# Decoder layer in fp32 on one core: the modulation rows of the first half move from VectorE to TensorE (four column strips), the low parts of h from GpSimd to VectorE, and TensorE gets 40 matmuls of constants to run early

## The chip, the cores and the metric

The kernel runs on one core of a Trainium2 chip. The metric is the device time in microseconds of one execution, as the median of several. TensorE (PE) has its own queue of instructions, and so have VectorE (DVE), ScalarE (ACT), GpSimd (POOL) and SyncE (SP), which here issues the loads. The engines meet only through semaphores, so the order of instructions on each engine is the order in which the Python code emits them.

## The reference

One layer over x of 1024 tokens by 1024 features, in float32. A conditioning vector c gives six rows of 1024 (shift, scale and gate, twice):

```python
mod = jax.nn.silu(c) @ w_ada[l] + b_ada[l]
shift1, scale1, gate1, shift2, scale2, gate2 = [m[:, None, :] for m in jnp.split(mod, N_MOD, axis=-1)]
h = rms_norm(x, norm_attn[l]) * (1.0 + scale1) + shift1
proj = h @ w_in[l]
...                                  # two attention groups, output projection, gate1, residual
h = rms_norm(x, norm_ffn[l]) * (1.0 + scale2) + shift2
ffn = (jax.nn.silu(h @ w_gate[l]) * (h @ w_up[l])) @ w_down[l]
x = x + gate2 * ffn
```

Only the part up to the first projections is touched: shift1 and scale1 (2048 columns of `w_ada`), the norm of x, h, and the first two of the 18 column tiles of `h @ w_in`.

## The kernel before, in words

Features lie on partitions: `x_in` is 8 chunks (j = 0 to 7) of 128 features by 1024 tokens. Each engine has one function, and the order in it is written by hand. A product in full precision is made of three fp32r matmuls: an operand is split into a high part (`hH`, `WH`, a copy rounded to fp32r) and a low part (`hL`, `WL`, the difference), and `three` (L1506 to L1508) adds high by high, high by low and low by high.

The stretch before the steady projections, called the prelude here, goes like this.

1. VectorE works out the angles of the rotary embedding (L938 to L962). ScalarE squares the chunks of x as they land (L569), and VectorE adds the squares (L980). PE turns the sums (L1537, fp32 transposes), VectorE reduces them (L1003, L1005), GpSimd raises the mean to the power -0.5 (L484), VectorE puts the result on diagonals (`diagonals`, L968), and PE spreads it over all partitions (`broadcast`, two fp32 matmuls of 128x512, L1531) into PSUM banks 6 and 7.
2. The 2048 columns of shift1 and scale1 come in four groups g = 0 to 3 of 512 columns, each good for two chunks of h. VectorE's `adaln1(g)` adds up seven of the eight products of `silu_c` with the weights (L990, L995: one tensor_scalar and six scalar_tensor_tensor of 128x512). PE's `adaln1(g)` sums over partitions and adds the eighth product, with 8 fp32 matmuls of one column (L1551, L1552). VectorE's `scale_shift(g)` (L1013, L1016) makes `mod1` and `a1` of it.
3. For each chunk j, VectorE multiplies x by the broadcast (L1021). ScalarE makes h with scale `a1` and bias `mod1` in place (L577), then `hH` as a copy of it (L579). GpSimd makes `hL` (L491).
4. PE runs the first two tiles of the projection against the chunks as they come (`half_chunk(0, ...)` on chunk n, `half_chunk(1, ...)` on chunk n - 3; 6 matmuls each). The remaining 16 tiles are whole (`proj_tile`, L1517), 48 matmuls each.

Behind the prelude GpSimd clears `acc2`, which lies over `x_in`, once all `hL` are made (L494). SyncE then loads the first piece of the other 4096 columns (`ada2`, L361), and VectorE's `ada_step` (L1039) takes it into `acc2`. On VectorE `ada_step(0)` stands between `wsplit(2)` and `wsplit(3)`; the latter makes `WL` of tile 3, for which PE waits at its start (semaphore `split_l`). Later in the layer come the attention groups and the FFN, which the change leaves as they are.

Of the kernel before, what the change touches and what calls it, by code (L numbers as in the profile page):

```python
# [15 lines left out]
F32 = mybir.dt.float32  # L16
# [7 lines left out]
P = 128  # L24
# [72 lines left out]
NM, NS = MH // 2 * NU, SBH // 2 * NU  # L97
BLOCKS = [NT - i for _, i in UNITS]
# [11 lines left out]
def build(nc, xT, cols_d, rows_d, grow_d, pos_d, ada1_d, ada2_d, win_d, qup_d, kvup_d, wout_d, gu_d, down_d, x2_d, t_d, out_d):  # L110
# [17 lines left out]
    silu_c = at("silu_c", [P, KD], F32, 6.125)  # L128
    mod1 = at("mod1", [P, 16], F32, 6.25)
# [134 lines left out]
    names = """small_in pool_const trig_args trig_done silu_c_done x_sq x_add x_turned stat_ms stat_r stat_diag stat_bc acc1_done mod1_mm a1_done  # L264
# [193 lines left out]
    def _(pool):  # L458
# [8 lines left out]

        fill(pool.memset(ident[:], 0.0))
# [82 lines left out]
    def _(act):  # L551
# [12 lines left out]
        A(silu_c[:], cols[:, C_C:C_C + KD], ACT.Silu).then_inc(sem["silu_c_done"], 1)  # L564
        for j in range(KD):
# [364 lines left out]
    def _(dve):  # L930
# [10 lines left out]
        for tt in range(NT):  # L941
            ch(V.tensor_scalar(ang[:, tt, 0, :], fr, pos_f[:, tt:tt + 1], None, ALU.mult))
            ch(V.tensor_scalar(ang[:, tt, 1, :], fr, pos_f[:, tt:tt + 1], None, ALU.mult))
# [38 lines left out]
        def adaln1(g, between=None):  # L982

            if g == 0:
                dve.wait_ge(sem["silu_c_done"], 1)
            if g >= 2:
                dve.wait_ge(sem["mod1_mm"], g - 1)
            dve.wait_ge(ada1_in[g], 16)
            a = acc1[g % 2]
            ch(V.tensor_scalar(a[:], ada1[:, g, 0, :], silu_c[:, 0:1], None, ALU.mult))  # L990
            for k in range(1, KD - 1):
                if k == 4 and between:
                    between()
# [12 lines left out]
        diagonals(0, 0, diag1)  # L1006
        adaln1(0)
# [491 lines left out]
    def _(pe):  # L1499
# [40 lines left out]
        def adaln1(g):  # L1540
# [6 lines left out]
            pe.wait_ge(sem["silu_c_done"], 1)  # L1547
            pe.wait_ge(sem["acc1_done"], g + 1)
            for m in range(4):
                w = slice(m * P, (m + 1) * P)  # L1550
                mm(ps[:, 4 + g % 2, m:m + 1], ada1[:, g, KD - 1, w], silu_c[:, KD - 1:KD], start=True, stop=False, skip_group_check=True)  # L1551
                last = mm(ps[:, 4 + g % 2, m:m + 1], acc1[g % 2][:, w], ones[:, 0:1], start=False, stop=True, skip_group_check=True)  # L1552
            last.then_inc(sem["mod1_mm"], 1)

        broadcast(0, diag1, 6)
        adaln1(0)


# [8 lines left out]
        for n in range(KD + LAG):  # L1567
            if n % 2 == 0 and n // 2 + 1 < KD // 2:
                adaln1(n // 2 + 1)
            if n < KD:  # L1570
                pe.wait_ge(sem["hL_done"], n + 1)
                for hf in range(2):
                    last = half_chunk(0, 0, hf, n, hH, hL)
                if n == KD - 1:
                    last.then_inc(sem["pe_tile"], 1)
            if n >= LAG:
                for hf in range(2):
                    last = half_chunk(1, 2, hf, n - LAG, hH, hL)
# [426 lines left out]
```

## Time and profile before

| | before |
|---|---|
| median of 3 runs | 1446.08 us (1443.46 to 1449.19) |
| profiled execution: its own time | 1443.19 us |
| its span, first to last instruction | 1441.2 us |
| PE busy | 1326.0 us, 92% |
| VectorE busy | 833.1 us, 58% |
| ScalarE busy | 547.3 us, 38% |
| GpSimd busy | 84.5 us, 6% |
| mean granted TensorE clock | 0.971 |

The span is shorter than the execution's time by 2.0 us, which lie around it. The profiled execution is 2.9 us under the median. In the page, "PEclk" is the clock granted to TensorE as a share of 2.4 GHz: 1.00 is that level, 0.50 is 1.2 GHz. Starts and durations of a timeline are in microseconds from the start of the span.

### The profile page before, as it was taken

What the parts mean: (1) busy time and instruction counts of PE and PEld (TensorE: products, weight loads), DVE (VectorE), ACT (ScalarE), POOL (GpSimd) and SP (SyncE); (2) the same over time, 40 slices, a digit from 0 to 9 for tenths busy, and PEclk for the clock granted to TensorE, in tenths of its full rate; (3) what the DMA queues carried; (4) which work ended last, traced back from release to release, by engine and by line L of the source; (5) the groups of instructions that cost most, each with busy time, mean ns of one, the idle gap of its engine ahead of it and who ended that gap; (6) DMA issues with size and microseconds to landing.
All of it is one profiled execution on the core that took longest, in us unless ns stands there. A gap on an engine that the chain in (4) does not pass through costs nothing.

```text
span 1441.2 us, 17190 instructions
## 1 busy us (share of the span) xinstructions
PE 1326.0 (92%) x6624; PEld 1107.3 (77%) x6624; DVE 833.1 (58%) x1225; ACT 547.3 (38%) x883; POOL 84.5 (6%) x82
## 2 busy tenths in 40 slices
PE   2899999887989898969989999999999999999998
PEld 1688878776877777768867788888888877887886
DVE  8633354477565998865368755666566633334333
ACT  3522312356444776852136333333333322323231
POOL 1600200132000000010000000000000000001001
PEclk9799999899999999979999999999999999999999
DMA  9053423000003323500122122222222225446443
GB/s 383 31 212 124 161 102 121 15 0 1 1 1 74 76 50 74 183 30 17 57 99 106 74 88 88 88 88 88 88 74 74 72 77 201 154 137 242 161 146 124
DMA packets 37404, 143.47 MB, mean 100 GB/s; under 512 B 4176, under 2 KB 4304, under 8 KB 35792
## 3 DMA queue, kind: packets, MB, share of 16 engines
q1 hardware_dynamic: 34992, 134.03, 27.5%
q0 software_dynamic: 2336, 8.39, 1.6%
q8 instruction: 52, 0.85, 0.3%
q14 instruction: 24, 0.20, 0.0%
HBM read 112.00 MB, written 19.92 MB: 92 GB/s over the span
## 4 chain that ended last, share of the span: by engine, by line
PE 71%; DVE 16%; issue 6%; ACT 3%; POOL 2%; DMA 1%; DVEq 0%; SPq 0%; ACTq 0%; POOLq 0%
PE ps L1905 26%; PE ps L1517 15%; PE ps L1506 8%; PE ps L1508 8%; PE ps L1507 8%; DVE left L1243 5%; PE ps L1713 2%; DVE acc L995 1%; DVE beta L1248 1%; PE ps L1702 1%; POOL rstd L508 1%; PE ps L1735 1%; PE ps L1722 1%; DMA t_spill_d<-tst 1%; PE ps L1822 1%
## 5 line engine op out<-in xcount | busy, mean ns | idle before, releaser
L1506 PE MATMUL ps<-TH,dWH 128*128 128x512 f32 x352 | 137.8, 391 | 7.2 <-DVE dWL L1474 6.3
L1507 PE MATMUL ps<-TL,dWH 128*128 128x512 f32 x352 | 137.7, 391 | 0.0
L1508 PE MATMUL ps<-TH,dWL 128*128 128x512 f32 x352 | 137.6, 391 | 0.0
L1905 PE MATMUL ps<-h2H,slH 128*128 128x512 f32 x320 | 124.6, 389 | 2.4 <-ACT s L900 2.4
L1905 PE MATMUL ps<-h2L,slH 128*128 128x512 f32 x320 | 124.5, 389 | 0.0
L1905 PE MATMUL ps<-h2H,slL 128*128 128x512 f32 x320 | 124.5, 389 | 0.0
L1472 DVE TENSOR_TENSOR TL<-traw,TH 128x512 fp32r<-128x512 f32 x44 | 30.5, 693 | 138.6 <-ACT TH L921 138.6
L883 ACT ACTIVATE slH<-ssum 128x512 fp32r<-128x512 f32 x80 | 50.4, 632 | 146.3 <-PE ps L1905 96.2
L1243 DVE TENSOR_TENSOR_SCAN left<-omb 128x127 f32<-128x127 f32 (+3 forms) x64 | 86.3, 1348 | 13.7 <-ACT omb L783 13.7
L921 ACT ACTIVATE TH<-traw 128x512 fp32r<-128x512 f32 x44 | 27.8, 631 | 168.9 <-PE ps L1508 156.8
L974 DVE TENSOR_TENSOR WL<-raw,WH 128x1024 fp32r<-128x1024 f32 x30 | 38.3, 1280 | 85.9 <-ACT WH L561 85.9
L1506 PEld LDWEIGHTS ps<-TH,dWH 128*128 128x128 f32 x352 | 66.5, 189 | 22.3 <-issue 7.1
L1517 PE MATMUL ps<-hH,WH 128*128 128x512 f32 x256 | 79.6, 392 | 0.0
L1517 PE MATMUL ps<-hL,WH 128*128 128x512 f32 x256 | 78.9, 389 | 0.0
L1517 PE MATMUL ps<-hH,WL 128*128 128x512 f32 x256 | 78.8, 389 | 0.0
L1508 PEld LDWEIGHTS ps<-TH,dWL 128*128 128x128 f32 x352 | 66.5, 189 | 13.8
L1507 PEld LDWEIGHTS ps<-TL,dWH 128*128 128x128 f32 x352 | 66.4, 189 | 13.8
L1735 PE MATMUL ps<-VS,wT 128*128 128x64 f32 x576 | 75.1, 278 | 0.0
L1735 PEld LDWEIGHTS ps<-VS,wT 128*128 128x128 f32 x576 | 73.4, 201 | 0.0
L1905 PEld LDWEIGHTS ps<-h2H,slH 128*128 128x128 f32 x320 | 60.1, 188 | 15.3 <-DVE slL L1419 2.8
L1905 PEld LDWEIGHTS ps<-h2L,slH 128*128 128x128 f32 x320 | 60.1, 188 | 12.4
L1905 PEld LDWEIGHTS ps<-h2H,slL 128*128 128x128 f32 x320 | 60.1, 188 | 12.4
(296 smaller groups left out, 3021.3 us busy)
## 6 DMA issues: line engine op xcount, KB each, us to landing
ada<-ada SPq DMA_DIRECT2D x12, 2048.0 KB, 8.1
draw<-down SPq DMA_DIRECT2D x44, 512.0 KB, 3.6
sraw<-gu SPq DMA_DIRECT2D x20, 1024.0 KB, 5.9
traw<-t_spill_d SPq DMA_DIRECT2D x44, 256.0 KB, 3.8
t_spill_d<-tst SPq DMA_DIRECT2D x20, 512.0 KB, 3.0
raw<-win SPq DMA_DIRECT2D x18, 512.0 KB, 3.7
x_in<-xT SPq DMA_DIRECT2D x4, 1024.0 KB, 8.5
headKH<-pairKH SPq DMA_DIRECT2D x16, 256.0 KB, 4.9
```

The lines of the kernel that those rows point to most:

```text
L883: A(slH[q][:], operand(u, q), ACT.Copy).then_inc(sem["g_h"], 1)
L921: A(TH[d % 2][:], traw[d % 2][:], ACT.Copy).then_inc(sem["th_done"], 1)
L974: V.tensor_tensor(WL[par % 2][:], raw[r % 2][:], WH[par % 2][:], ALU.subtract).then_inc(sem["split_l"], 1)
L1243: V.tensor_tensor_scan(left[v % 2][:, 1:n], omb[v % 2][:, 0:n - 1], omb[v % 2][:, 0:n - 1], 1.0, ALU.mult, ALU.bypass).then_inc(sem["s_sca ...
L1472: V.tensor_tensor(TL[d % 2][:], traw[d % 2][:], TH[d % 2][:], ALU.subtract).then_inc(sem["tl_done"], 1)
L1506: mm(out, lh, rh, start=first, stop=False)
L1507: mm(out, lh, rl, start=False, stop=False)
L1508: return mm(out, ll, rh, start=False, stop=last)
L1517: last = mm(ps[:, b + hf, :], l[s][:, j * P:(j + 1) * P], r[:, j, 512 * hf:512 * hf + 512], start=(j == 0 and k == 0), stop=(j == KD - 1 a ...
L1713: last = mm(ps[:, 6 + v % 2, 0:VD], pmT[v % 2][:, k * P:(k + 1) * P], VM[:, qt + k, (2 * i + e) * VD:(2 * i + e + 1) * VD], start=(k == 0) ...
L1735: last = mm(ps[:, bank, c:c + SBD], wT[v % 2][:, k * P:(k + 1) * P], VS[:, qt + k, (2 * i + e) * SBD:(2 * i + e + 1) * SBD], start=(k == 0 ...
L1905: last = mm(ps[:, Q_BANK[q], :], l[q][:, w], r[:, c, :], start=(c == 0 and k == 0 and q not in (Q_G2, Q_S4)), stop=(c == 3 and k == 2), sk ...
```

## The change

- VectorE no longer adds up the modulation rows. PE does it (`mod1_rows(g)`): eight fp32 matmuls, whose stationary operand `silu_w` has 32 columns per k (silu(c) in the first, zeros in the others) and whose moving operand is 128x512 of the weights. Matmul k writes the 32 partitions 32*(k % 4) onward of one PSUM bank, so it uses one of four column strips of the array, two matmuls to a strip. VectorE copies the bank to SBUF (`mod1_copy`), and PE sums over partitions with four fp32 matmuls of one column (`mod1_columns`), where there were eight.
- `hL` is made by VectorE (`h_low`) instead of GpSimd.
- ScalarE makes `hH` straight from x with scale and bias, and h after it, with the same scale and bias; before, `hH` was a copy of h.
- The 16 small instructions for the angles become two. The eight small ones for the first diagonals become two halves, and each half of the broadcast has a wait and a signal of its own. `wsplit(0)` moves behind the reduction, `wsplit(1)` behind the diagonals.
- PE runs 40 bf16 matmuls of 128x128 on a constant (`WARM`) between the transposes and the first `mod1_rows`.
- In the loop of the first two tiles, PE no longer takes the three kinds of products of a chunk together: the four matmuls that need only `hH` come as soon as that is there, then `mod1_rows`, the chunk of tile 1, `mod1_columns`, and last the two with `hL`.

```diff
+WARM = 40
...
-        for j in range(KD):
-            pool.wait_ge(sem["hH_done"], j + 1)
-            nc.gpsimd.tensor_tensor(hL[:, j, :], x_in[:, j, :], hH[:, j, :], ALU.subtract).then_inc(sem["hL_done"], 1)
...
+            A(hH[:, j, :], x_in[:, j, :], ACT.Identity, scale=a1[:, j:j + 1], bias=mod1[:, j:j + 1]).then_inc(sem["hH_done"], 1)
             A(x_in[:, j, :], x_in[:, j, :], ACT.Identity, scale=a1[:, j:j + 1], bias=mod1[:, j:j + 1]).then_inc(sem["h_done"], 1)
-            act.wait_ge(sem["h_done"], j + 1)
-            A(hH[:, j, :], x_in[:, j, :], ACT.Copy).then_inc(sem["hH_done"], 1)
...
+        def mod1_copy(g):
+
+            dve.wait_ge(sem["ada_part"], g + 1)
             if g >= 2:
                 dve.wait_ge(sem["mod1_mm"], g - 1)
...
+            V.tensor_copy(acc1[g % 2][:], ps[:, 4 + g % 2, :]).then_inc(sem["acc1_done"], 1)
...
+        def normalize(j):
+            V.tensor_tensor(x_in[:, j, :], x_in[:, j, :], pair(6), ALU.mult).then_inc(sem["xr_done"], 1)
+
+        def h_low(j):
+            dve.wait_ge(sem["hH_done"], j + 1)
+            dve.wait_ge(sem["h_done"], j + 1)
+            V.tensor_tensor(hL[:, j, :], x_in[:, j, :], hH[:, j, :], ALU.subtract).then_inc(sem["hL_done"], 1)
+
+        mod1_copy(0)
+        dve.wait_ge(sem["stat_bc"], 2)
+        normalize(0)
+        scale_shift(0)
+        normalize(1)
         for g in range(KD // 2):
...
+            if 2 * g + 2 < KD:
+                normalize(2 * g + 2)
+            h_low(2 * g)
             if g + 1 < KD // 2:
...
+                mod1_copy(g + 1)
+                normalize(2 * g + 3)
+            h_low(2 * g + 1)
+            if g + 1 < KD // 2:
+                scale_shift(g + 1)
...
+        def mod1_rows(g):
+
             if g == 0:
                 pe.wait_ge(sem["stat_ms"], 1)
+                pe.wait_ge(sem["silu_c_done"], 2)
             if g >= 2:
                 pe.wait_ge(sem["a1_done"], g - 1)
             pe.wait_ge(ada1_in[g], 16)
...
+            for k in range(KD):
+                c = k % 4
+                last = mm(ps[32 * c:32 * c + 32, 4 + g % 2, :], silu_w[:, k, :], ada1[:, g, k, :], start=(k < 4), stop=(k >= 4))
+            last.then_inc(sem["ada_part"], 1)
```

On PE, from the end of the transposes to the second group, the row of instructions before was this (`diag` is the diagonal, `ada` the weights of the modulation, `acc` the row sums; two numbers behind a name are the program's buffer number):

```order
L1537 MATMUL ps<-ident,sqs 128x128 x7
L1531 MATMUL ps<-diag_97,ones 128x512 [waits stat_diag]
L1531 MATMUL ps<-diag_97,ones 128x512
L1551 MATMUL ps<-silu_c,ada_90 128x1 [waits silu_c_done,acc1_done,ada1_in0,stat_ms]
L1552 MATMUL ps<-ones,acc_91 128x1
...
L1551 MATMUL ps<-silu_c,ada_90 128x1 [waits silu_c_done,acc1_done,ada1_in1,split_l]
L1552 MATMUL ps<-ones,acc_92 128x1
...
L1506 MATMUL ps<-hH,WH_79 128x512 [waits hL_done]
L1507 MATMUL ps<-hL,WH_79 128x512
L1508 MATMUL ps<-hH,WL_81 128x512
```

and of the change it is this:

```order
L1541 MATMUL ps<-ident,sqs 128x128 x7
L1565 MATMUL ps<-identb 128x128 x40
L1554 MATMUL ps<-ada_91,silu_w 32x512 [waits ada1_in0,silu_c_done,stat_ms]
L1554 MATMUL ps<-ada_91,silu_w 32x512 x7
L1569 MATMUL ps<-diag_98,ones 128x512 [waits stat_diag] x2
L1561 MATMUL ps<-ones,acc_92 128x1 [waits acc1_done]
L1561 MATMUL ps<-ones,acc_92 128x1 x3
L1587 MATMUL ps<-hH,WH_80 128x512 [waits hH_done,split_l]
L1587 MATMUL ps<-hH,WH_80 128x512
L1587 MATMUL ps<-hH,WL_82 128x512 x2
L1554 MATMUL ps<-ada_91,silu_w 32x512 [waits ada1_in1]
L1554 MATMUL ps<-ada_91,silu_w 32x512 x7
```

The constants and eight matmuls of the rows now stand ahead of the broadcast, and the rows of group 1 stand behind the first chunk's `hH` products, where the one-column matmuls of group 1 stood ahead of everything of chunk 0.

On VectorE, one turn of the loop over groups was this before (`mod` and `a` are `mod1` and `a1`):

```order
L1021 TENSOR_TENSOR x_in<-x_in,ps 128x1024 x2
L990 TENSOR_SCALAR acc_91<-ada_90,silu_c 128x512 [waits ada1_in2,mod1_mm]
L995 SCALAR_TENSOR_TENSOR acc_91<-ada_90,silu_c,acc_91 128x512 [waits dve] x3
L1013 TENSOR_TENSOR mod_60<-ps,cols 128x2x2 [waits mod1_mm]
L1016 SCALAR_TENSOR_TENSOR a_61<-mod_60,cols 128x2 [waits dve]
L995 SCALAR_TENSOR_TENSOR acc_91<-ada_90,silu_c,acc_91 128x512 [waits dve] x3
```

and is this with the change:

```order
L1009 TENSOR_TENSOR x_in<-x_in,ps 128x1024
L1014 TENSOR_TENSOR hL<-x_in,hH 128x1024 [waits h_done,hH_done]
L986 COPY acc_92<-ps 128x512 [waits mod1_mm,ada_part]
L1009 TENSOR_TENSOR x_in<-x_in,ps 128x1024
L1014 TENSOR_TENSOR hL<-x_in,hH 128x1024 [waits h_done,hH_done]
L1003 TENSOR_TENSOR mod_61<-ps,cols 128x2x2 [waits mod1_mm]
L1006 SCALAR_TENSOR_TENSOR a_62<-mod_61,cols 128x2 [waits dve]
```

The seven accumulations are gone. A copy that waits for PE and two `hL` that wait for ScalarE have come in, and the scale and shift of the next group stand at the end of the turn.

## Rows read from the trace of the kernel before

**Rows 1.** The page: shares of the chain that ended last, by engine

```profile
PE 71%; DVE 16%; issue 6%; ACT 3%; POOL 2%; DMA 1%; DVEq 0%; SPq 0%; ACTq 0%; POOLq 0%
```

**Rows 2.** Windows of PE alone: stretch, length, busy (instructions), granted clock, DMA share, GB/s

```profile
33.40:36.00 2.60, 1.12 (x6) 0.51 0.96 410
...
47.00:50.40 3.40, 1.92 (x13) 0.99 0.00 0
50.40:57.00 6.60, 6.60 (x21) 0.51 0.01 2
...
61.70:77.00 15.30, 15.25 (x67) 1.00 0.24 75
```

**Rows 3.** Timeline, 3 to 38 us: start, duration, engine, line, instruction, count

```profile
3.78 0.24 DVE L942 TENSOR_SCALAR ang<-rows,pos_f 128x32 f32<-128x32 f32 x1
...
10.54 9.20 DVE L980 TENSOR_TENSOR sqs<-sqs,sq 128x1024 f32<-128x1024 f32 x7
...
17.18 1.06 ACT L569 ACTIVATE sq<-x_in 128x1024 f32<-128x1024 f32 x1 [0.27 <-DVE sqs L980]
...
19.89 1.94 PE L1537 MATMUL ps<-ident,sqs 128*128 128x128 f32 x8 [19.89 <-DVE sqs L980]
...
23.51 1.68 POOL L484 TENSOR_TENSOR rms<-ms,nhalf 128x8 f32<-128x8 f32 x1 [20.48 <-DVE ms L1005]
...
26.93 3.50 PE L1531 MATMUL ps<-diag,ones 128*128 128x512 f32 x4 [5.10 <-DVE diag L968]
...
37.12 0.16 DVE L1016 SCALAR_TENSOR_TENSOR a<-mod,cols 128x2 f32<-128x2 f32 x1
```

**Rows 4.** Groups by form, 0 to 80 us: count, busy, mean ns, idle before

```profile
L995 DVE SCALAR_TENSOR_TENSOR acc<-ada,silu_c,acc 128x512 f32<-128x512 f32 x24 | 22.0, 916 | 0.7
...
L577 ACT ACTIVATE x_in<-x_in,mod,a 128x1024 f32<-128x1024 f32 x8 | 9.9, 1235 | 27.5 <-DVE a L1016 27.5
L1021 DVE TENSOR_TENSOR x_in<-x_in,ps 128x1024 f32<-128x1024 f32 x8 | 9.4, 1213 | 0.0
```

**Rows 5.** Timeline, 59 to 87 us

```profile
59.41 0.36 PE L1552 MATMUL ps<-ones,acc 128*128 128x1 f32 x2
59.64 0.36 PE L1551 MATMUL ps<-silu_c,ada 128*128 128x1 f32 x2
...
61.42 0.29 DVE L1016 SCALAR_TENSOR_TENSOR a<-mod,cols 128x2 f32<-128x2 f32 x1
...
69.03 3.53 POOL L494 MEMSET acc<- 128x4096 f32 x1
...
76.84 0.62 PE L1517 MATMUL ps<-hH,WH 128*128 128x512 f32 x2
...
80.61 4.49 DVE L1039 SCALAR_TENSOR_TENSOR acc<-ada,silu_c,acc 128x4096 f32<-128x4096 f32 x1 [6.63 <-DMA ada<-ada]
85.01 1.22 DVE L974 TENSOR_TENSOR WL<-raw,WH 128x1024 fp32r<-128x1024 f32 x1
```

**Rows 6.** Timeline of PE at full clock: four fp32 matmuls of 128x512, then bf16

```profile
209.21 3.59 PE L1531 MATMUL ps<-diagl,ones 128*128 128x512 f32 x8
...
393.15 0.23 PE L1676 MATMUL ps<-mask_mla,identb 128*128 128x128 bf16 x1
393.21 0.71 PE L1702 MATMUL ps<-ident,pm 128*128 128x128 f32 x5
```

**Rows 7.** Groups by form, whole span: the nearest row to VectorE's new copy

```profile
L1182 DVE COPY pmT<-ps 128x384 f32<-128x384 f32 x8 | 4.5, 558 | 0.1
```

**Rows 8.** What reads or writes x_in and ada: issues (from, to), time to landing (min/median/max)

```profile
L349 SPq DMA_DIRECT2D x_in<-xT x4: 434/469/688, 2.1 to 3.6; - x4
...
DMA to landing us min/median/max: 5.4/8.5/11.5
...
L353 SPq DMA_DIRECT2D ada<-ada x4: 457/668/1201, 5.4 to 7.3; - x4
...
DMA to landing us min/median/max: 17.3/24.3/30.6
```

More of the change, by code:

```diff
@@ L940, in _ @@
         fr = rows[:, R_FREQ:R_FREQ + HALF]
[L941 to L943 removed]
+        for c in range(2):
+            ch(V.tensor_tensor(ang[:, :, c, :], fr.unsqueeze(1).broadcast_to([P, NT, HALF]), pos_f[:].unsqueeze(2).broadcast_to([P, NT, HALF]), ALU.mult))
         ch.sync()
@@ L1005, in _ @@
         V.tensor_scalar(ms[:, 0, :], rss[:], 1.0 / D, EPS, ALU.mult, ALU.add).then_inc(sem["stat_ms"], 1)
-        diagonals(0, 0, diag1)
-        adaln1(0)
+        wsplit(0, 0)
+        dve.wait_ge(sem["stat_r"], 1)
+        for hf in range(2):
+            t = slice(4 * hf, 4 * hf + 4)
+            V.tensor_tensor(diag1[:, t, :], ident[:].unsqueeze(1).broadcast_to([P, 4, P]), rms[:, 0, t].unsqueeze(2).broadcast_to([P, 4, P]), ALU.mult).then_inc(sem["stat_diag"], 1)
+        wsplit(1, 1)
         def scale_shift(g):
@@ L1546, in adaln1, with mod1_columns @@
             pe.wait_ge(ada1_in[g], 16)
-            pe.wait_ge(sem["silu_c_done"], 1)
+            for k in range(KD):
+                c = k % 4
+                last = mm(ps[32 * c:32 * c + 32, 4 + g % 2, :], silu_w[:, k, :], ada1[:, g, k, :], start=(k < 4), stop=(k >= 4))
+            last.then_inc(sem["ada_part"], 1)
+        def mod1_columns(g):
             pe.wait_ge(sem["acc1_done"], g + 1)
             for m in range(4):
-                w = slice(m * P, (m + 1) * P)
-                mm(ps[:, 4 + g % 2, m:m + 1], ada1[:, g, KD - 1, w], silu_c[:, KD - 1:KD], start=True, stop=False, skip_group_check=True)
-                last = mm(ps[:, 4 + g % 2, m:m + 1], acc1[g % 2][:, w], ones[:, 0:1], start=False, stop=True, skip_group_check=True)
+                last = mm(ps[:, 4 + g % 2, m:m + 1], acc1[g % 2][:, m * P:(m + 1) * P], ones[:, 0:1], start=True, stop=True)
             last.then_inc(sem["mod1_mm"], 1)
-        broadcast(0, diag1, 6)
-        adaln1(0)
+        for _ in range(WARM):
+            mm(ps[:, 0, 0:P], identb[:], identb[:], start=True, stop=True)
+        mod1_rows(0)
+        for hf in range(2):
+            pe.wait_ge(sem["stat_diag"], hf + 1)
+            mm(ps[:, 6 + hf, :], ones[:], diag1[:, 4 * hf:4 * hf + 4, :].rearrange("p t n -> p (t n)"), start=True, stop=True).then_inc(sem["stat_bc"], 1)
+        mod1_columns(0)
         def in_pair(t0, i):
@@ L1567, in _ @@
         for n in range(KD + LAG):
-            if n % 2 == 0 and n // 2 + 1 < KD // 2:
-                adaln1(n // 2 + 1)
+            if n < KD:
+                w = slice(n * P, (n + 1) * P)
+                pe.wait_ge(sem["hH_done"], n + 1)
+                for k, l in enumerate((WH, WL)):
+                    for hf in range(2):
+                        mm(ps[:, hf, :], l[0][:, w], hH[:, n, 512 * hf:512 * hf + 512], start=(n == 0 and k == 0), stop=False)
+            if n % 2 == 0 and n // 2 + 1 < KD // 2:
+                mod1_rows(n // 2 + 1)
+            if n >= LAG:
+                for hf in range(2):
+                    last = half_chunk(1, 2, hf, n - LAG, hH, hL)
+            if n % 2 == 0 and n // 2 + 1 < KD // 2:
+                mod1_columns(n // 2 + 1)
             if n < KD:
@@ L1572, in _ @@
                 for hf in range(2):
-                    last = half_chunk(0, 0, hf, n, hH, hL)
+                    last = mm(ps[:, hf, :], WH[0][:, w], hL[:, n, 512 * hf:512 * hf + 512], start=False, stop=(n == KD - 1))
                 if n == KD - 1:
                     last.then_inc(sem["pe_tile"], 1)
-            if n >= LAG:
-                for hf in range(2):
-                    last = half_chunk(1, 2, hf, n - LAG, hH, hL)
         last.then_inc(sem["pe_tile"], 1)
```

35 lines of the change are left out of this document (8 added, 27 removed).

## The prediction

> **What bounds the kernel now.** I read the shares of the chain that ended last first: TensorE holds 71% of it and VectorE 16% [rows 1]. The windows of PE and the timeline of the first 90 us then say where that differs. From 61.75 us on PE goes without a gap, 67 matmuls in 15.25 us, 0.227 us each [rows 2], and it hands over to the whole tiles at 76.84 us [rows 5]. Those are bound by PE and the change leaves them alone. So what the change can move is the moment 76.84, and what hangs on it a little later.
>
> Ahead of 61.75 us VectorE is the bound. `a1` of group 0 is ready at 37.28 us and that of group 3 at 61.71 us [rows 3, 5]. That is 24.4 us over three groups, 8.1 us each on the mean (9.8 us for the first two, less for the last, whose scale and shift stand early). In a group VectorE makes six scalar_tensor_tensor at 0.916 us on the mean and two products at 1.213 us [rows 4], with a tensor_scalar and two small ones. Idle time before these rows is nearly nothing, so VectorE is at work all through. At 61.7 us PE still has 66 of the 96 matmuls of tiles 0 and 1 before it. This is a backlog, and it matters below: it was 15.1 us of work from 61.75 to 76.84.
>
> **The new operation, and its price R.** The eight matmuls of `mod1_rows` are fp32 with 512 moving columns. At full clock four such matmuls are recorded as 8 pieces in 3.59 us [rows 6], the drain of the last included, so a piece takes 0.427 us and a matmul 0.854 us. At 26.93 us two of them took 3.50 us [rows 3], that is 0.85 us a piece: half speed. No row of before has a matmul that uses 32 columns of the array. The bounds for R at full clock are:
> - one after another, as the broadcasts go: 8 x 0.854 = 6.83 us
> - all four strips at once: two rounds of 0.854 us, 1.7 us, and 1.9 us with some filling.
>
> I take a value between: every fp32 matmul is two pieces, all rows of PE show starts in program order, and the second piece of a strip cannot start before the first of the same strip is done. If a later strip may not pass it, its first piece runs beside the earlier strip's second, so two pieces are in flight: 8 x 0.427 + 0.427 = 3.84 us. I keep both ends for the range.
>
> The Trainium skill (TensorE: Matmul & The Clock Gate, Part 3: Packing small matmuls) says that matmuls start and end strictly in order, and that three column tiles of 512 columns gave 2.38 times the speed. The first speaks for 3.84 us. By the second, taken to four tiles as 3.1 times, an estimate from that page, R would be 2.2 us and the kernel near 1437 us. No run here shows either yet.
>
> **Up to `a1` of group 0.** The 16 small instructions, 0.24 us each [rows 3], become two of 256 columns, at most 0.56 us each (a copy of 384 [rows 7]). The first add of squares can start up to 1 us sooner than 10.54 us. The last chunk of x lands at 3.6 + 11.5 = 15.1 us [rows 8]. Two squares (1.06 us each) and one add (1.22 us, as every difference of 1024 columns [rows 5]) behind it, with their waits, end near 18.7 us. The seven adds ended at 19.74 us [rows 3], so this gains 1.0 us. The transposes (1.94 us), reduction and rsqrt follow at the same distance: `rms` at 24.2 us instead of 25.19 [rows 3]. `wsplit(0)` lies beside GpSimd's 1.68 us and costs nothing. The two halves of the diagonals (0.69 each, as the copy below) end at 25.6 us. `wsplit(1)` ends at 26.8 us, before the rows are done, hidden too.
>
> PE starts the 40 constants at 20.9 us. A bf16 matmul of 128x128 is followed after 0.06 us at full clock [rows 6]: 2.4 us at full clock, 4.8 us at half. I take 25.2 us for their end, since PE was idle before. The weights of group 0 landed at 5.4 + 17.3 = 22.7 us, the last group's at 7.3 + 30.6 = 37.9 us [rows 8], in time for every group here. Then:
> - rows 3.84 us to 29.04
> - broadcast, 2 x 0.854 to 30.75
> - end of PE's pipe and semaphore 0.27 (a matmul of 0.227 us is recorded as 0.39)
> - `normalize(0)` 1.21 to 32.2
> - scale and shift 0.35 to 32.6 us.
>
> The copy and the one-column matmuls (four at 0.225 us [rows 5], 0.9 us) lie beside the broadcast and `normalize(0)`. So `a1` of group 0 comes at 32.6 us, 4.7 us earlier.
>
> **One group.** The path goes: `a1`, ScalarE's `hH` 1.24 us [rows 4] with 0.08 for the semaphore, four matmuls 0.91, rows R, pipe 0.27, copy 0.69 (0.558 us for 384 columns [rows 7], carried to 512), `normalize` 1.17, `h_low` 1.17, scale and shift 0.35, semaphore 0.1. This is 5.98 + R. The one-column matmuls (0.9 + 0.27) lie beside the two VectorE instructions that follow the copy. ScalarE needs 4 x 1.24 = 4.96 us a group, VectorE 2 x 1.17 + 2 x 1.17 + 0.69 + 0.35 = 5.7 us, so neither is the bound. With R = 3.84 a group takes 9.82 us and `a1` of group 3 comes at 32.6 + 29.5 = 62.0 us, no earlier than the 61.71 of before.
>
> **From there to the end of tile 1.** PE has a smaller backlog now. Behind `a1` of group 3 stand 1.3 us for `hH` of chunk 6, 42 matmuls (the rest of chunks 6 and 7 of tile 0 and chunks 3 to 7 of tile 1), 9.5 us, and about 0.5 us of waits on the last `hL`: 11.3 us instead of 15.1. Tile 1 ends at 73.3 us, 3.5 us earlier than 76.84.
>
> **What is late next.** GpSimd clears `acc2` only when the last `hL` is made, in 3.53 us, then the load of `ada2` takes 8.05 us, from 72.56 to 80.61 us, `ada_step(0)` 4.49 us, and only behind it comes `wsplit(3)`, done at 86.23 us [rows 5]. PE wants that at the end of tile 2: 76.84 + 48 x 0.227 = 87.7 us. Before there were 1.5 us to spare. Now the last `hL` comes at 62.0 + 0.1 + 4 x 1.24 + 0.1 + 1.2 = 68.4 us (ScalarE makes two pairs behind `a1`). Then 3.6 + 8.05 + 4.49 + 1.2 us bring `WL` of tile 3 at 85.8 us, and tile 2 ends at 73.3 + 10.9 = 84.2 us. PE waits 1.5 us. After that the steps follow the tiles again.
>
> The sum is 3.5 - 1.5 = 2.0 us faster. On the profiled execution's 1443.19 us this gives 1441.2 us. The median of the runs stands 2.9 us above that execution, so I predict 1446.08 - 2.0 = **1444 us**. What a measurement of this kernel can tell from no change is about 0.5%, 7.2 us.
>
> **The rivals.**
> 1. *Four strips at once, R = 1.9.* `a1` of group 0 at 30.65 us, groups of 7.88 us, group 3 at 54.3, tile 1 at 65.6, and the wait of 1.5 us: 9.7 us faster, 1436.4 us. For it: strips share no columns and no output partitions. Against it: program order, and two pieces to each matmul. The estimate of 1437 by the page's speedup ends near it.
> 2. *The strips don't overlap, R = 6.83.* This is the one on the other side. `a1` of group 0 at 35.6 us, groups of 12.81 us, group 3 at 74.0, tile 1 at 85.3: 10 us slower, 1456 us. For it: all 6,000 and more other matmuls go one by one. It decides from R near 4.5: each us of R costs 1 + 3 = 4 us, so the gain of 2.0 is gone at R = 4.34.
> 3. *PE at the lower clock in the loop.* The granted clock was at 0.51 from 33.4 and again from 50.4 us, each time after a stretch in which PE had been idle or had done one-column matmuls (in 47.0 to 50.4 us it was busy 1.92 of 3.40 us) [rows 2]. Now each group has 0.9 us of one-column work and gaps of 1.1 us for the copy and 1.2 us for `hH`. Behind `mod1_columns(0)` the gap is 2 us. A group at half speed adds 3.84 + 0.91 = 4.75 us, all three 14 us: 1458 us. Against it: the rest of each group is dense. The constants speak only of the start. Without the 2.4 GHz level at 25.2 us the first rows and the broadcast cost 5.5 us more.
>
> **How the numbers follow.** Two strips at a time: 0.45, near 1444, own range 1439 to 1449. Four at once or close to it (R under 3): 0.28. No overlap: 0.14. Low clock in most groups: 0.08. The remaining 0.05 is for something else, on either side. Two in ten may lie outside: the range goes from 1434 (the first rival and its fill at nothing) to 1455 us. Faster by over 0.5% needs R near 2.5 or less, 0.28 of the first rival and a little of the rest: 0.30. Slower by over 0.5% is rivals 2 and 3: 0.21. Within: 0.49.
>
> **What would show it.** In the profile of the change: the time from the first to the last piece of eight matmuls with `silu_w` (1.9, 3.8 or 6.8 us); whether pieces of neighbouring strips overlap; `a1` at 32.6 us and then every 9.8 us; the first whole tile at 73.3 us; VectorE idle before the copy in each group, waiting for PE; PE idle for 1.5 us before tile 3, until `WL`. The granted clock should be at 1.00 from 25 us on. The prediction is wrong if R is far from 3.84, if the clock falls in the loop, or if ScalarE's `hH` with scale and bias is slower than 1.24 us.

## The result, and the profile after

| | runs | median us | lowest to highest | profiled run: time, span, granted clock |
|---|---|---|---|---|
| before | 6 | 1448.18 | 1443.46 to 1450.22 | 1443.19, 1441.2, 0.971 |
| changed | 6 | 1435.22 | 1431.80 to 1438.66 | 1431.80, 1430.0, 0.983 |

The ratio is 0.9916, 95% interval 0.9892 to 0.9939. The kernel is 12 us (0.84%) faster by the ratio, which is more than the 0.5% that can be told from no change. The forecast was 1444 us and no change. So the forecast of no change failed, although the measured time lies inside the range of 1434 to 1455 us. It lies there because the range reached down to the first rival (1436.4 us, from a base 2.1 us lower), and not because the expected mechanism came true.

The step R is decided by the timeline of the changed kernel from 20 to 31 us (start, duration, engine, line, instruction, count, and in brackets the idle time before with its releaser):

```profile
20.17 1.94 PE L1541 MATMUL ps<-ident,sqs 128*128 128x128 f32 x8 [20.17 <-DVE sqs L979]
21.90 4.03 PE L1565 MATMUL ps<-identb 128*128 128x128 bf16 x40
23.73 2.51 POOL L487 TENSOR_TENSOR rms<-ms,nhalf 128x8 f32<-128x8 f32 x1 [20.47 <-DVE ms L991]
25.86 0.16 PEld L1554 LDWEIGHTS ps<-ada,silu_w 128*32 128x32 f32 x8
25.86 1.92 PE L1554 MATMUL ps<-ada,silu_w 128*32 128x512 f32 x16
...
26.32 0.13 PEld L1554 LDWEIGHTS ps<-ada,silu_w 128*32 128x32 f32 x4 [0.30 <-issue]
26.75 0.13 PEld L1554 LDWEIGHTS ps<-ada,silu_w 128*32 128x32 f32 x4 [0.30 <-issue]
27.72 1.98 PE L1569 MATMUL ps<-diag,ones 128*128 128x512 f32 x4
...
29.54 0.95 PE L1561 MATMUL ps<-ones,acc 128*128 128x1 f32 x8
31.07 0.16 DVE L1006 SCALAR_TENSOR_TENSOR a<-mod,cols 128x2 f32<-128x2 f32 x1
```

The eight matmuls of `mod1_rows` (16 pieces, L1554) take 1.92 us, where 3.84 us had been taken. The weight loads (PEld) show how: eight at 25.86, then four at 26.32 and four at 26.75, 0.46 and 0.43 us apart, about one piece's 0.427 us. So four pieces of 512 columns run at once, one in each strip, and the pieces of a strip follow each other without a gap. `a1` of group 0 is ready at 31.23 us. In [rows 3] it was 37.28.

Then the groups. From the same timeline, the rows of groups 1 to 3 and their copies:

```profile
34.69 3.64 PE L1554 MATMUL ps<-ada,silu_w 128*32 128x512 f32 x16
38.40 0.69 DVE L986 COPY acc<-ps 128x512 f32<-128x512 f32 x1 [3.37 <-PE ps L1554]
41.46 0.16 DVE L1006 SCALAR_TENSOR_TENSOR a<-mod,cols 128x2 f32<-128x2 f32 x1
44.13 1.92 PE L1554 MATMUL ps<-ada,silu_w 128*32 128x512 f32 x16
46.12 0.69 DVE L986 COPY acc<-ps 128x512 f32<-128x512 f32 x1 [0.70 <-PE ps L1554]
49.19 0.16 DVE L1006 SCALAR_TENSOR_TENSOR a<-mod,cols 128x2 f32<-128x2 f32 x1
52.09 1.92 PE L1554 MATMUL ps<-ada,silu_w 128*32 128x512 f32 x16
```

From one `a1` to the next it takes 10.4, 7.7 and 8.0 us. The prediction's sum for a group, 5.98 + R, gives 7.90 with the measured R. The last two groups agree with it. Group 1 doesn't: its rows took 3.64 us. The windows of PE tell why (stretch, length, busy, granted clock, DMA share, GB/s):

```profile
25.86:27.72 1.86, 1.86 (x19) 1.00 0.99 423
29.54:32.71 3.17, 0.95 (x9) 0.91 1.02 434
32.71:38.40 5.69, 5.62 (x20) 0.50 0.96 397
38.40:69.08 30.68, 28.27 (x148) 0.99 0.07 18
```

After 3.17 us in which PE had 0.95 us of one-column work, TensorE's clock is at the 1.2 GHz level (0.50) for the 5.69 us of group 1, and back at 2.4 GHz behind it. That is the third rival, in one group of three and for 2.5 us instead of 4.75.

Last, what was late behind `a1` of group 3 (57.14 us), again from the timeline. The rows of before are in [rows 5]:

```profile
63.42 3.54 POOL L493 MEMSET acc<- 128x4096 f32 x1 [37.18 <-DVE hL L1014]
69.08 0.62 PE L1521 MATMUL ps<-hH,WH 128*128 128x512 f32 x2
69.28 1.03 ACT L585 ACTIVATE lowT<-ps 128x1024 f32<-128x1024 f32 x1 [2.04 <-PE ps L1512]
74.93 4.49 DVE L1043 SCALAR_TENSOR_TENSOR acc<-ada,silu_c,acc 128x4096 f32<-128x4096 f32 x1 [7.36 <-DMA ada<-ada]
79.34 1.22 DVE L973 TENSOR_TENSOR WL<-raw,WH 128x1024 fp32r<-128x1024 f32 x1
80.70 0.70 PE L1521 MATMUL ps<-hH,WH 128*128 128x512 f32 x2 [0.58 <-DVE WL L973]
92.01 1.03 ACT L585 ACTIVATE lowT<-ps 128x1024 f32 x1 [9.78 <-PE ps L1521]
```

PE goes over to the whole tiles at 69.08 us instead of 76.84. Then it waits for `WL` of tile 3: from the eviction of tile 2 to that of tile 3 are 11.75 us (80.26 to 92.01), to the next one 10.88, a loss of 0.87 us. At tile 3's eviction, at 98.90 us in before, the gain is 6.9 us.

VectorE was busy 54.41 us up to 61.71 us in before. In the changed kernel it is 39.66 us, although it now makes `hL` too. Its share of the chain that ended last is 14% (16% in [rows 1]), PE's 72%.

### The profile page after: what moved, and what is told of

Same layout as the page of the kernel before. It is cut to its first block, busy times and chain, and to the rows that moved or that the text cites. A ratio compares the mean times of both kernels' runs of the same rounds, so it can differ in the third digit from the quotient of the medians.

```text
span 1430.0 us, 17295 instructions
## 1 busy us (share of the span) xinstructions
PE 1321.2 (92%) x6696; PEld 1096.7 (77%) x6696; DVE 820.3 (57%) x1189; ACT 547.9 (38%) x884; POOL 66.2 (5%) x75
## 4 chain that ended last, share of the span: by engine, by line
PE 72%; DVE 14%; issue 6%; ACT 3%; DMA 2%; POOL 2%; DVEq 0%; SPq 0%; ACTq 0%; POOLq 0%
PE ps L1927 26%; PE ps L1521 14%; PE ps L1510 8%; PE ps L1512 8%; PE ps L1511 8%; DVE left L1247 5%; PE ps L1735 2%; DVE beta L1252 1%; PE ps L1724 1%; POOL rstd L507 1%; PE ps L1744 1%; PE ps L1554 1%; DMA t_spill_d<-tst 1%; PE ps L1844 1%; DMA x_in<-xT 1%
## 5 line engine op out<-in xcount | busy, mean ns | idle before, releaser
L1247 DVE TENSOR_TENSOR_SCAN left<-omb 128x127 f32<-128x127 f32 (+3 forms) x64 | 86.3, 1349 | 12.4 <-ACT omb L783 12.4
L1757 PE MATMUL ps<-VS,wT 128*128 128x64 f32 x576 | 71.8, 271 | 0.0
L1757 PEld LDWEIGHTS ps<-VS,wT 128*128 128x128 f32 x576 | 70.0, 193 | 0.0
```

What stands on the lines that cost most here:

```text
L1247: V.tensor_tensor_scan(left[v % 2][:, 1:n], omb[v % 2][:, 0:n - 1], omb[v % 2][:, 0:n - 1], 1.0, ALU.mult, ALU.bypass).then_inc(sem["s_sca ...
L1757: last = mm(ps[:, bank, c:c + SBD], wT[v % 2][:, k * P:(k + 1) * P], VS[:, qt + k, (2 * i + e) * SBD:(2 * i + e + 1) * SBD], start=(k == 0 ...
```

## The experiments

Times are medians. The ratios are to runs of before on the same chip, whose medians lie between 1447.6 and 1448.9 us. Below, "tile 1" is the start of its eviction, the `lowT` row at 69.28 us in the changed kernel (77.04 in before), and "tile 3" likewise (92.01, 98.90). The constant matmuls that some kernels add write to a part of `ps` that holds nothing at that time.

### How many strips

**e1_one_by_one**, no strips, the whole array for each matmul:

```
-    silu_w = at("silu_w", [P, KD, 32], F32, 138)
+    silu_w = at("silu_w", [P, KD, P], F32, 138)
-                c = k % 4
-                last = mm(ps[32 * c:32 * c + 32, 4 + g % 2, :], silu_w[:, k, :], ..., start=(k < 4), stop=(k >= 4))
+                last = mm(ps[:, 4 + g % 2, :], silu_w[:, k, :], ..., start=(k == 0), stop=(k == KD - 1))
```

> The changed kernel with one edit: the stationary operand of the rows has 128 columns (silu(c) in the first, zeros in the others), so each of the eight matmuls uses the whole width and all write the same partitions. Theory (the gain comes from four strips in flight at once; each us of R, the time of eight such matmuls, costs one in the start and one in each of three groups): R goes from 1.9 to 6.8 us at full clock, the first whole tile starts at 69.1 + 4 x 5.0 = 89 us, the kernel takes about 20 us more than the changed one and is slower than before by 7 to 10 us. Rival (strips do not matter, the gain comes from VectorE's freed time): R stays near 1.9 to 2.5, tile 2 starts at 69 to 71 us.

1452.61 us (10 runs), ratio 1.0035 [1.0018, 1.0051]: slower than before. PE's timeline of this kernel:

```profile
25.08 7.08 PE L1553 MATMUL ps<-ada,silu_w 128*128 128x512 f32 x16
32.00 1.88 PE L1568 MATMUL ps<-diag,ones 128*128 128x512 f32 x4
```

R is 6.9 us (25.08 to 32.00). `a1` of group 0 is ready at 35.41 us, where the second rival's sum had 35.6. Tile 1 ends at 87.32 us, 18.0 later than in the changed kernel, for 5.0 us of R. By "4 us for each us of R" it should be 20. The profiled changed kernel had lost 2.5 us in its group 1 to the clock (10.4 for 7.9), and this one 1.5 (14.4 for the sum's 12.9), so the sum becomes 19. This one's transposes also started 0.7 us sooner (19.44 for 20.17), which leaves 18.3.

The slowdown against before is 4.5 us, less than the 7 to 10 expected. This kernel has every other edit of the change, from the angles to the order of the loop. So with the rows on PE, all of them together don't make the kernel faster without the strips. What one does by itself was tried for `hL` only (e7, e10).

**e2_two_strips**, two strips of 64 columns:

```
-    silu_w = at("silu_w", [P, KD, 32], F32, 138)
+    silu_w = at("silu_w", [P, KD, 64], F32, 138)
-                c = k % 4
-                last = mm(ps[32 * c:32 * c + 32, ...], ..., start=(k < 4), stop=(k >= 4))
+                c = k % 2
+                last = mm(ps[64 * c:64 * c + 64, ...], ..., start=(k < 2), stop=(k >= KD - 2))
```

> The changed kernel with two column strips of 64 columns in place of four of 32. Theory (all strips of a round run at once): four rounds of 0.854 us, R = 3.4 us at full clock, tile 2 starts near 69.1 + 4 x 1.6 = 75.5 us, about 6 us more than the changed kernel. Rival (only two pieces are ever in flight, and R = 1.9 comes from something else): R stays at 1.9 with two strips and the time is that of the changed kernel.

1443.98 us (10 runs), ratio 0.9973 [0.9953, 0.9993]; `a1` of group 0 at 32.23 us, tile 1 at 74.41. PE's timeline:

```profile
25.14 3.65 PE L1554 MATMUL ps<-ada,silu_w 128*64 128x512 f32 x16
28.72 1.99 PE L1569 MATMUL ps<-diag,ones 128*128 128x512 f32 x4
```

This kernel has by its construction the overlap that the prediction gave to four strips, two pieces in flight. R is 3.6 us and `a1` of group 0 is 0.4 us from the forecast of 32.6. The median is the forecast's 1444, but from a base of 1448.1 and not 1446.1: the gain is some 4 us, where the forecast had 2.0.

**e12_same_strip_pairs**, four strips, but the two matmuls of a strip follow each other in the program. If starts in program order blocked the strips behind, this order would be the worst one.

```
-                c = k % 4
-                last = mm(..., start=(k < 4), stop=(k >= 4))
+                c = k // 2
+                last = mm(..., start=(k % 2 == 0), stop=(k % 2 == 1))
```

> The changed kernel with one edit: matmul k of the rows goes to strip k // 2 instead of k % 4, so the two of a strip follow each other in program order. Theory (matmuls start in program order and one that waits for its strip blocks those behind it): only neighbours of different strips overlap, R becomes at least 2 x 0.854 + 3 x 0.854 = 4.3 us and at most 5.6 us instead of 1.9, tile 2 starts 10 us or more later than in the changed kernel. Rival (each strip takes its own matmuls in its own time): R stays at 1.9 and nothing changes.

1433.45 us (4 runs), ratio 0.9911 [0.9881, 0.9942]. PE's timeline, with the loads:

```profile
24.84 0.18 PEld L1554 LDWEIGHTS ps<-ada,silu_w 128*32 128x32 f32 x8
24.84 1.94 PE L1554 MATMUL ps<-ada,silu_w 128*32 128x512 f32 x16
25.30 0.15 PEld L1554 LDWEIGHTS ps<-ada,silu_w 128*32 128x32 f32 x4 [0.28 <-issue]
26.72 1.98 PE L1569 MATMUL ps<-diag,ones 128*128 128x512 f32 x4
```

1.94 us against 1.92: the order makes no difference, where blocking would have made it at least 4.3 us. R over the three layouts is 6.9, 3.6 and 1.9 us for one, two and four strips. It goes with the number of strips, and not with their order.

### TensorE's clock

**e3_no_warm** leaves the 40 constants out:

```
-WARM = 40
+WARM = 0
```

> The changed kernel without the 40 constants of 128x128 ahead of the first rows. Theory (they buy the clock for the first rows and the broadcast): the first rows take 3.6 us instead of 1.9 and the broadcast 3.5 instead of 2.0, but they start 2 us sooner, when the mean square is ready; a1 of group 0 comes 1 to 2 us later and tile 2 starts at 70 to 73 us. Rival (the constants are not needed, the transposes before them are enough): a1 of group 0 comes earlier or at the same time, tile 2 at 67 to 69 us.

1438.54 us (5 runs, 1433.25 to 1442.34), ratio 0.9918 [0.9893, 0.9943]. PE's timeline:

```profile
22.62 3.64 PE L1554 MATMUL ps<-ada,silu_w 128*32 128x512 f32 x16 [1.63 <-DMA ada<-ada]
...
34.20 2.37 PE L1554 MATMUL ps<-ada,silu_w 128*32 128x512 f32 x16
```

The rows run at half speed, but they start 3.2 us sooner, as soon as their weights have landed, because no constants stand ahead of them. `a1` of group 0 comes at 30.75 us instead of 31.23, and tile 1 at 67.55.

That doesn't mean that the constants are worth nothing. In this profile x landed sooner, and with it the whole start. The first square of x, first in the changed kernel, then here:

```profile
8.46 1.06 ACT L570 ACTIVATE sqs<-x_in 128x1024 f32<-128x1024 f32 x1 [4.30 <-DMA x_in<-xT]
```

```profile
7.41 1.06 ACT L570 ACTIVATE sqs<-x_in 128x1024 f32<-128x1024 f32 x1 [3.08 <-DMA x_in<-xT]
```

The transposes follow this square after 11.6 to 11.7 us in every profile of the changed kernel and its variants, so here they start 1.1 us sooner (19.05 for 20.17). From their start to `a1` of group 0 are 11.70 us here, and 10.6 to 11.5 us in the seven profiles that have the constants and four strips. So the constants buy 0.2 to 1.1 us. The prediction had them at 5.5 us, and had left out that without them the rows start earlier and lie beside the wait for `rms`.

**e4_fill** puts 36 constants into the gap behind `mod1_columns(0)`, ahead of the group in which the clock was at 0.50:

```
         mod1_columns(0)
+        for _ in range(FILL):      # FILL = 36
+            mm(ps[:, 0, 0:P], identb[:], identb[:], start=True, stop=True)
```

> The changed kernel with 36 more constants behind the one-column matmuls of group 0, in the gap of 2.2 us in which PE waits for hH of chunk 0. Theory (the sparse stretch of PE from 29.5 to 32.7 us is what drops the clock for group 1, where the rows took 3.64 us): the rows of group 1 take 1.9 us, the granted clock stays at 1.00, tile 2 starts 2.5 to 3 us earlier, near 66.3 us. Rival (the fall to half has another cause, such as the narrow matmuls of the rows themselves): the rows of group 1 still take 3.6 us and tile 2 starts at 69 us.

1433.43 us (4 runs), ratio 0.9897 [0.9871, 0.9923]. PE's timeline:

```profile
29.97 2.17 PE L1573 MATMUL ps<-identb 128*128 128x128 bf16 x36
...
33.42 1.92 PE L1555 MATMUL ps<-ada,silu_w 128*32 128x512 f32 x16
```

Group 1 takes 7.8 us instead of 10.4, at a granted clock of 1.00, and tile 1 ends at 66.31 us, 3.0 sooner. The median is 1.8 us below that of the changed kernel, within the spread of either. By itself this profile doesn't show that the fill did it, as the next run says.

**a1_after_again** is the changed kernel once more, on another chip:

> The changed kernel again, unchanged, for more runs of it beside the next kernel on the same chip. Both theories expect 1433 to 1436 us, and a first whole tile that starts at 68 to 69.5 us.

1434.75 us (6 runs), ratio 0.9916 [0.9897, 0.9935]. PE's timeline, and below it the window of group 1 (columns: stretch, length, then busy time of PE, its loads, VectorE, ScalarE and GpSimd, then granted clock, DMA share, GB/s):

```profile
28.88 1.05 PE L1561 MATMUL ps<-ones,acc 128*128 128x1 f32 x8 [0.26 <-DVE acc L986]
31.81 0.70 PE L1587 MATMUL ps<-hH,WH 128*128 128x512 f32 x2 [1.88 <-ACT hH L578]
32.90 1.92 PE L1554 MATMUL ps<-ada,silu_w 128*32 128x512 f32 x16
```

```profile
32.70:38.50 5.80, 4.99 (x34) 2.68 (x32) 4.80 (x7) 2.65 (x4) 0.00 (x0) 1.00 0.96 398
```

The same program keeps the clock at 1.00 this time. Tile 1 ends at 65.75 us, 3.5 us before the first profile and sooner than the 68 to 69.5 expected, and 0.15 us from the 65.6 of the first rival. So the drop in group 1 comes in some runs and not in others. It is the usual case, though: of the eight profiles with four, two or one strips and without the fill, six have it (all but a1 and e12), and the two with the fill, e4 and e8, don't. The rows of group 1 took 3.64 us in the first profile, 2.37 in e3, 3.37 in e7 and 2.38 in e11, where those of group 2 took 1.92; in e1 it was 8.72 for 7.03 us, in e2 4.66 for 3.65. PE's idle time ahead of the first `hH` product is not the same in all. It is 2.2 us in five of the six (2.23 in the first profile), and 1.88 us in a1 and e12. But e7, with 1.88 us too, drops to 1.2 GHz. Two profiles are few, so that the fill prevents the drop is likely and not shown.

### VectorE and the rest

**e7_low_gpsimd** gives the low parts of `h` back to GpSimd and leaves all else as in the changed kernel:

```
+        for j in range(KD):
+            pool.wait_ge(sem["h_done"], j + 1)
+            nc.gpsimd.tensor_tensor(hL[:, j, :], x_in[:, j, :], hH[:, j, :], ALU.subtract).then_inc(sem["hL_done"], 1)
...
-            V.tensor_tensor(hL[:, j, :], x_in[:, j, :], hH[:, j, :], ALU.subtract).then_inc(sem["hL_done"], 1)
```

> The changed kernel, but GpSimd makes the low parts of h again. Theory (the rows on PE alone carry the gain in the loop over groups, and the chain through VectorE gets shorter by the two h_low of 1.17 us, while an instruction of VectorE takes longer whenever GpSimd runs): groups take 6.5 to 7.5 us instead of 7.8, but GpSimd needs 4.8 us a group and ends last, hL of chunk 7 comes later; tile 2 starts within 1.5 us of the changed kernel's 69.1. Rival (the low parts on VectorE are what carries the gain): tile 2 starts at 73 us or later.

1435.28 us (4 runs), ratio 0.9926 [0.9901, 0.9952]; tile 1 at 65.87 us, as in a1 (65.75). The groups take 8.4, 7.3 and 7.9 us, not the 6.5 to 7.5 expected; the first of them met the lower clock (its rows took 3.37 us), which a1 didn't. Without that, tile 1 would come some 1.5 us sooner, an estimate from 3.37 less 1.92. In the median it makes no difference that can be told which of the two engines makes `hL`.

**e10_before_low_vector** does that part alone in the kernel before:

```
-        for j in range(KD):
-            pool.wait_ge(sem["hH_done"], j + 1)
-            nc.gpsimd.tensor_tensor(hL[:, j, :], x_in[:, j, :], hH[:, j, :], ALU.subtract).then_inc(sem["hL_done"], 1)
...
+            for j in (2 * g, 2 * g + 1):
+                dve.wait_ge(sem["hH_done"], j + 1)
+                V.tensor_tensor(hL[:, j, :], x_in[:, j, :], hH[:, j, :], ALU.subtract).then_inc(sem["hL_done"], 1)
```

> The kernel before, but VectorE makes the low parts of h, behind the row sums of each next group. Theory (before, VectorE is the bound of the prelude): 2.4 us more work of VectorE in each group, partly given back since GpSimd no longer slows it (six accumulations at 0.92 us on the mean against 0.76 alone); groups take 10.5 to 11.5 us, tile 2 starts at 78 to 82 us, 1 to 5 us slower than before. Rival (GpSimd's hL was the slow part): tile 2 starts at 72 to 75 us, faster than before.

1448.07 us (10 runs), ratio 1.0007 [0.9993, 1.0020]. Of its VectorE and ScalarE rows, two `a1` and tiles 1 and 3:

```profile
37.13 0.16 DVE L1012 SCALAR_TENSOR_TENSOR a<-mod,cols 128x2 f32<-128x2 f32 x1
48.32 0.16 DVE L1012 SCALAR_TENSOR_TENSOR a<-mod,cols 128x2 f32<-128x2 f32 x1
81.70 1.03 ACT L581 ACTIVATE lowT<-ps 128x1024 f32<-128x1024 f32 x1 [3.41 <-PE ps L1507]
103.56 1.03 ACT L581 ACTIVATE lowT<-ps 128x1024 f32 x1 [8.90 <-PE ps L1516]
```

A group takes 11.2 us instead of 9.8 and tile 1 ends 4.7 us later, as VectorE was the bound there. So this part of the change, taken alone, lengthens the prelude. Yet the median isn't later by that. It is the first sign that medians and single profiles of the prelude don't agree to better than some 4 us.

**e8_all** joins e4's fill with `scale_shift` of the next group ahead of the second `h_low`, and does without the clearing of `acc2`, by a first step that multiplies only:

```
-            h_low(2 * g + 1)
             if g + 1 < KD // 2:
                 scale_shift(g + 1)
+            h_low(2 * g + 1)
...
-        pool.memset(acc2[:], 0.0).then_inc(sem["ada_acc"], 1)
+        pool.sem_inc(sem["ada_acc"], 1)
...
+            if isinstance(step, int) and step == 0:
+                V.tensor_scalar(acc2[:], ada2[:], silu_c[:, 0:1], None, ALU.mult).then_inc(sem["ada_acc"], 1)
```

> The changed kernel with three edits: 36 constants behind the first one-column matmuls; scale and shift of the next group ahead of the second h_low; no clearing of acc2 (the first step writes it without adding), so that the load of ada2 starts as soon as the last hL is made. Theory: 2.2 us from the clock of group 1, 1 us in each of three groups from the order, and the wait of 0.9 us before tile 3 gone: tile 3 ends near 86.5 us where the changed kernel had it at 92.0, the kernel takes about 5.5 us less than the changed one and its ratio to before is near 0.988. Rival (the order gives nothing since the one-column matmuls come too late, and the load stays the bound of tile 3): 2 to 3 us less only.

1434.52 us (6 runs), ratio 0.9905 [0.9886, 0.9924]. Its first step on VectorE, and tiles 2 and 3 on ScalarE:

```profile
67.00 2.35 DVE L1044 TENSOR_SCALAR acc<-ada,silu_c 128x4096 f32<-128x4096 f32 x1 [3.68 <-DMA ada<-ada]
76.00 1.03 ACT L586 ACTIVATE lowT<-ps 128x1024 f32 x1 [9.01 <-PE ps L1524]
86.88 1.03 ACT L586 ACTIVATE lowT<-ps 128x1024 f32 x1 [8.90 <-PE ps L1524]
```

The wait before tile 3 is gone (10.88 us between these two) and tile 3 is 5.1 us ahead of the changed kernel's first profile. The median is 0.7 us lower. It has the shortest prelude of all, but its time can't be told from the changed kernel's; the 5.5 us expected didn't show.

**b1_before_again** and **b2_before_third** are the kernel before, profiled on two more chips.

> The kernel before, unchanged, for a second profile of it. Theory (the profiled run of before lies 5 us under the median because its later stages met a better granted clock than usual, the prelude being the same): the first whole tile starts again at 77.0 us within 0.5, and in a run of 1446 to 1449 us the extra 4 to 6 us lie behind 260 us. Rival (the prelude itself is longer in the usual run): it starts at 80 us or later.

> The kernel before, unchanged, for a third profile. Expected again: tile 3 ends at 98.9 us within 0.5, and what this run differs by from the other two lies behind 260 us.

They gave 1445.85 and 1449.25 us. In b1 the prelude is that of [rows 3, 5] to 0.02 us (tile 3 at 98.88), and 2.7 us more span lie behind it. In b2 tile 3 comes at 100.85 us, 2 us later, all of it ahead of tile 1 and against the expectation. Behind tile 3 the stages that no edit touches vary too. One window of PE of before, then of b2, then of the changed kernel:

```profile
468.60:602.60 134.00, 121.11 (x920) 0.97 0.38 95
```

```profile
471.60:610.50 138.90, 127.16 (x920) 0.93 0.36 92
```

```profile
460.30:593.20 132.90, 119.80 (x921) 0.99 0.38 96
```

The stage from 468.60 us (471.60, 460.30) has the same work in all of them, 920 or 921 matmul records. It takes 134.0 us at a clock of 0.97, 138.9 at 0.93 and 132.9 at 0.99. In e3, which differs from the changed kernel only in the 40 constants near 22 us, it took 139.3 us at 0.93.

What lies behind tile 3 can be summed for all fourteen profiles, as the span less the start of tile 3. It is 1342.3, 1345.0 and 1346.4 us in the three of before and 1340.2 in e10, 1343.5 on the mean. In the ten of the changed kernel and its variants it goes from 1338.0 (the first profile) to 1349.4 us (e3), 1343.2 on the mean.

**e11_delayed** asks whether the later stages are quicker because they start sooner. It puts 128 constants, 7.3 us, between tiles 1 and 2, so that they start near where before starts them (tile 3 at 96.30 us, 98.90 in before):

```
         last.then_inc(sem["pe_tile"], 1)
+        for _ in range(DELAY):     # DELAY = 128
+            mm(ps[:, 6, 0:P], identb[:], identb[:], start=True, stop=True)
         repeat(pe, 2, lambda i: in_pair(2, i))
```

> The changed kernel with 128 more constants (7.1 us at full clock) on PE between tiles 1 and 2, so that everything behind the prelude starts at about the moment at which it did before. The gain of the medians (12 to 13 us) is larger than what the two profiles show at the end of tile 3 (6.9 us). Theory (the rest belongs to the granted clock of the later stages and depends on when they start): the stages behind tile 3 take again what they take in the kernel before, some 1347 us, and the kernel lies at 1446 to 1448 us. Rival (the rest is the change's own or chance between runs, and does not depend on the start): they keep the 1341 us of the changed kernel, and the kernel lies 6 to 7 us above it, at 1441 to 1443 us.

1441.83 us (12 runs), ratio 0.9952 [0.9935, 0.9969]: 7.1 us over the changed kernel on that chip, for 7.3 us put in (of which the wait before tile 3, 0.8 us in a1, is given back). Behind tile 3 lie 1340.6 us, as in a1 (1341.6). So a delay here reaches the end within the spread of the medians, and there is no sign that the later stages are quicker for starting sooner.

## Where the prediction failed and where it held, step by step

**The failed step is R**, in "The new operation, and its price R", and with it the forecast of no change. The prediction said that starts go in program order, that the second piece of a strip cannot start before its first is done, and that "if a later strip may not pass it", two pieces are in flight, R = 3.84. A later strip does pass it. R is 1.86 to 1.92 us, the end of the bounds called "all four strips at once". e12 shows that this doesn't hang on the order of the strips: there the second matmul of each strip stands ahead of the next strip's first, and R is 1.94 us all the same. e2 shows that the price of 3.84 us belongs to two strips (3.6). The choice between the bounds rested on a rule read from matmuls that all used the whole array, where a second one has no free columns to go to. Such rows can't tell order from occupancy.

The Trainium skill (TensorE: Matmul & The Clock Gate, Part 3: Packing small matmuls) was used on both sides. Its strict order of start and end, which spoke for 3.84, didn't bind between strips here: e12's R of 1.94 us leaves no room for it. The estimate worked out from its speedup, R 2.2 us, came near the measured 1.9. The strips gave 6.9 / 1.9 = 3.6 times by these runs, where that estimate had 3.1.

**What hung on R was right.** The sum 5.98 + R for a group gives 7.90 us, measured 7.7 to 8.0. `a1` of group 0 by the sum and the measured R comes at 30.65 us; in a1 it is ready at 30.32 us, in the first profile at 31.23. "Each us of R costs 4 us" gave 20 us for e1 and 18.0 came, by profiles that differ in the clock of group 1 and in the start; with both counted the sum is 18.3. With R = 1.9 the forecast's own terms gave a gain of 9.7 us. At tile 3 a1 has 10.5 and the first profile 6.9, with 2.5 of the difference from the clock. The medians have 12 to 13. The 1436.4 us are only 1.2 above the measured median because the base was 2.1 us too low, which is luck.

**The start.** In the first profile the transposes start at 20.17 us, not 1.0 sooner than the 19.89 of [rows 3] but later, and `rms` is ready at 26.24 us against the 24.2 forecast. The shorter work is there: from the first square of x to the transposes are 11.6 to 11.7 us in all profiles of the change and its variants, 12.4 to 13.1 in those of before and e10. What took it back is the landing of x, with the first square at 7.41 to 8.49 us in the former and 7.08 to 7.53 in the latter. The prediction had no term for that, and why x lands later isn't shown. GpSimd's power took 2.51 us instead of 1.68 beside `wsplit(0)`, which had been called free. In the first profile it is hidden, as the first diagonals are made (from 26.28 us on) while PE is still at the rows (to 27.72 us). The 40 constants end at 25.9 us instead of 25.2 (24.9 in a1, from 21.42 on).

**Tile 1 to tile 3.** From `a1` of group 3 (57.30 us) to the first whole tile are 11.8 us, 11.3 foreseen. The wait before tile 3 was foreseen at 1.5 us for R = 3.84 and also in the first rival; it is 0.87 us in the first profile, in which `a1` had come late, and in a1 0.82 us (11.70 less 10.88). Over the variants it is 0.6 (e12) to 1.7 us (e3). e8 shows that it goes with the clearing of `acc2` and the first step.

**The clock.** The third rival happened, but in one group and for 2.5 us at most with four strips: in the first profile, not in a1. With the fill (e4, e8) it wasn't seen. The constants at the start were priced at 5.5 us and are worth 0.2 to 1.1 us by the profiles, since they also keep the rows from starting at 22.6 us. The medians say nothing on it: e3's ratio to before is 0.9918, the changed kernel's 0.9916.

**What stays open.** The prelude gives 6.9 to 10.5 us by the profiles (tile 3 at 92.01 and 88.43, against 98.90), the medians differ by 12 to 13 us. That is less of a gap than it seems. Tile 3 of before comes at 99.5 us on the mean of its three profiles, that of the changed kernel and e12 at 89.6, a difference of 9.9 us. The interval of the first ratio goes from 8.8 to 15.6 us and so holds it. Behind tile 3 the two kinds of kernel take the same on the mean (1343.5 and 1343.2 us), though single profiles differ by up to 11 us, about 6 of them in the one stage whose granted clock is 0.93 to 0.99. So nothing here shows that the changed kernel meets a higher clock more often, and a rest of 2 to 3 us may be chance. What makes the later clock vary from run to run wasn't settled.

## What to carry to other kernels

Eight narrow fp32 matmuls in column strips of the array ran side by side here, and their time went down with the number of strips (6.9, 3.6, 1.9 us for one, two, four), whatever their order. When a rule of order is read from full-width instructions, ask first whether those rows could have shown anything else.

An operation that stands in a chain once per group is priced by its multiplicity (here four), so its two bounds gave -9.7 and +10 us and the chance should have been put between them, not on a third value that only a chain of assumptions supported.

Work put in to keep the clock up is worth only what it saves less what it delays: the constants ahead of rows whose inputs were there bought 0.2 to 1.1 us, not 5.5. And two profiles are compared from a common event on, not from zero: here the landing of x moved the whole start by up to 1.1 us.

## What the runs showed of the hardware that was not expected

- Both pieces of an fp32 matmul overlap with those of the other strips: 16 pieces of 0.427 us in 1.92 us, with loads for four pieces at a time every 0.43 to 0.46 us. In e12, whose program has the two matmuls of a strip one behind the other, it is 1.94 us.
- The same program met a granted clock of 0.50 or of 1.00 for its group 1, behind a gap of about 3 us with some one-column matmuls in it (0.50 in the first profile, 1.00 in a1). With 36 bf16 matmuls of 128x128 in that gap (2.17 us) it was at 1.00 in both profiles, e4 and e8.
- The power of 128x8 on GpSimd took 2.51 us beside a VectorE product of 128x1024 (the first profile), 1.68 us in [rows 3].
- VectorE took 2.35 us for `acc2` of 128x4096 by a tensor_scalar, and 4.49 us by the scalar_tensor_tensor that also adds (e8).
